# Second layer norms, embedding gates and expert sums with tokens on partitions, and every expert weight split finished on DVE

## The reference, cut to what matters

```python
x = _layer_norm(ALPHA * x + merged @ w_out[i], ln1_g[i], ln1_b[i])      # first norm
if i == 0:
    f = _swiglu(x, ffn_w1[0], ffn_w3[0], ffn_w2[0])                     # dense, 2816 hidden
else:
    f = moe_swiglu(x, ...)       # 8 experts of 3584 hidden, 2 per token, weighted by gates
ple = jax.nn.sigmoid(x @ w_ple_gate[i]) * (p[i] @ w_ple[i])             # embedding and its gate
x = _layer_norm(ALPHA * x + f + ple, ln2_g[i], ln2_b[i])                # second norm
```

## Time and profile before

| | |
|---|---|
| time, median of 3 runs | 2164.01 us (2162.94 to 2166.07) |
| profiled execution: its time | 2165.63 us |
| profiled execution: span from first to last instruction | 2163.8 us |
| TensorE busy | 2093.7 us, 97% of the span |
| VectorE busy | 1458.6 us, 67% |
| ScalarE busy | 966.4 us, 45% |
| GpSimd busy | 350.3 us, 16% |
| mean granted TensorE clock | 0.985 of full speed |
| bytes moved | 553.32 MB, 256 GB/s over the span |

### The profile page before, as it was taken

How to read it: one execution, slowest core, us unless ns; L and a number is a source line. 1 busy time by engine, 2 the same in 40 slices (tenths; PEclk the granted TensorE clock), 3 DMA queues, 4 the chain that set the end, 5 groups by cost and what they waited for, 6 DMA issues and landing times.

```text
span 2163.8 us, 28939 instructions
## 1 busy us (share of the span) xinstructions
PE 2093.7 (97%) x11722; PEld 1801.5 (83%) x11722; DVE 1458.6 (67%) x1415; ACT 966.4 (45%) x1029; POOL 350.3 (16%) x99
## 2 busy tenths in 40 slices
PE   8999999999999989999999999999999979989998
PEld 8877899998877878888888888888888858768998
DVE  4332677664333588898888888888988942346765
ACT  0133210002133257777877777777777732341000
POOL 1001200000001132222232222232224310100000
PEclk9999999999999989999999999999999999999999
DMA  9633579652613468999999999999999963324520
GB/s 350 216 132 104 164 260 326 231 175 79 235 64 117 156 242 328 369 384 385 370 388 367 385 369 388 366 380 368 386 385 386 375 212 122 117 78 156 195 98 20
DMA packets 175854, 553.32 MB, mean 256 GB/s; under 512 B 9248, under 2 KB 97952, under 8 KB 132368
## 3 DMA queue, kind: packets, MB, share of 16 engines
q1 hardware_dynamic: 166928, 517.55, 65.3%
q10 hardware_dynamic: 6912, 25.02, 2.8%
q0 software_dynamic: 1920, 9.40, 1.2%
HBM read 528.09 MB, written 23.59 MB: 255 GB/s over the span
## 4 chain that ended last, share of the span: by engine, by line
PE 91%; DVE 6%; issue 1%; ACT 1%; DMA 0%; DVEq 0%; SPq 0%; ACTq 0%
PE act_ps L1036 26%; PE dve_ps L1061 13%; PE act_ps L859 12%; PE act_ps L964 9%; PE dve_ps L964 9%; PE dve_ps L859 8%; PE job_ps L997 6%; DVE weights_rest L2059 3%; PE job_ps L1044 1%; PE job_ps L911 1%; PE job_ps L930 1%; PE act_ps L1172 1%; PE job_ps L942 1%; PE dve_ps L1377 1%; PE job_ps L1377 1%
## 5 line engine op out<-in xcount | busy, mean ns | idle before, releaser
L2059 DVE TENSOR_TENSOR weights_rest<-weight_ring,expert_short 128x2048 fp32r<-128x2048 f32 x280 | 775.2, 2809 | 110.2 <-ACT expert_short L1545 110.2
L1545 ACT ACTIVATE expert_short<-weight_ring 128x2048 fp32r<-128x2048 f32 x336 | 641.2, 1918 | 104.4 <-PE act_ps L1036 70.7
L748 POOL TENSOR_TENSOR weights_rest<-weight_ring,expert_short 128x2048 fp32r<-128x2048 f32 x56 | 269.2, 4808 | 677.2 <-ACT expert_short L1545 677.2
L1036 PE MATMUL act_ps<-expert_short,tokens_short 128*128 128x512 f32 x896 | 356.2, 397 | 3.9 <-DVE tokens_rest L2069 3.9
L1036 PE MATMUL act_ps<-weights_rest,tokens_short 128*128 128x512 f32 x896 | 351.0, 392 | 0.0
L1036 PE MATMUL act_ps<-expert_short,tokens_rest 128*128 128x512 f32 x896 | 350.8, 392 | 0.0
L1450 ACT ACTIVATE arena_mla<-act_ps 128x256 f32<-128x256 f32 (+1 forms) x80 | 32.6, 407 | 409.1 <-PE act_ps L964 345.5
L1036 PEld LDWEIGHTS act_ps<-expert_short,tokens_short 128*128 128x128 f32 x896 | 169.5, 189 | 38.2 <-DVE weights_rest L2059 4.2
L1036 PEld LDWEIGHTS act_ps<-expert_short,tokens_rest 128*128 128x128 f32 x896 | 169.4, 189 | 36.7
L1036 PEld LDWEIGHTS act_ps<-weights_rest,tokens_short 128*128 128x128 f32 x896 | 169.6, 189 | 33.8
L1988 DVE TENSOR_TENSOR weights_rest<-weight_ring,ffn_weights_short 128x2048 fp32r<-128x2048 f32 x66 | 151.3, 2292 | 2.3
(11 more groups left out here) (325 smaller groups left out, 3718.9 us busy)
## 6 DMA issues: line engine op xcount, KB each, us to landing
weight_ring<-in_moe_w SPq DMA_DIRECT2D x336, 1024.0 KB, 7.2
weight_ring<-in_w_in SPq DMA_DIRECT2D x44, 1024.0 KB, 7.4
weight_ring<-in_ffn_w SPq DMA_DIRECT2D x32, 1024.0 KB, 6.9
weight_ring<-in_w_out SPq DMA_DIRECT2D x12, 1024.0 KB, 6.3
weight_ring<-in_w_gate SPq DMA_DIRECT2D x11, 1024.0 KB, 5.4
weight_ring<-in_w_up SPq DMA_DIRECT2D x11, 1024.0 KB, 8.0
weight_ring<-in_w_down SPq DMA_DIRECT2D x10, 1024.0 KB, 7.1
weight_ring<-in_w_ple_gate SPq DMA_DIRECT2D x8, 1024.0 KB, 6.5
```

The costliest lines, as they stand in the source:

```text
L748: nc.gpsimd.tensor_tensor(ring_lo[slot][:, half], ring[:, slot, half], shorts[u % SHORTS][:, :], ALU.subtract)\
L1036: m = nc.tensor.matmul(bank[0:CAP, :], a[:, 4 * c + k, :], w[:, k, :], start=(c == k == i == 0), stop=(c == 1 and k == 3 and i == 2))
L1545: nc.scalar.activation(shorts[u % SHORTS][:, :], ring[:, slot, half], ACT.Copy).then_inc(moe_w_short, 1)
L2059: V.tensor_tensor(ring_lo[slot][:, half], ring[:, slot, half], shorts[u % SHORTS][:, :], ALU.subtract)\
```

## The change

Three things are laid out with tokens on partitions, two tiles of 128 tokens x 1024 features, in the same buffer `z` (now also viewed as `z_rows`):

1. The `w2` units of the dense network (`swiglu(..., by_rows=True)`) and the embedding gate (`ple_rows`) have the tokens stationary and 512 weight columns moving, 24 matmuls a unit. The embedding product is 4 tiles of 128 x 512 instead of 8 of 128 x 256. ACT scales `x`, turned by TensorE (`turn_x`, which layer 1 had already for its token rows), by ALPHA into `z_rows`; DVE adds gate times embedding.
2. The second norm (`rows_norm`) takes its statistics on DVE with `bn_stats` and `bn_aggr` along the row, ACT makes the root of a 128 x 1 column, DVE normalises, and TensorE turns the rows back (`turn_rows`, 16 transposes). Gain and bias are applied while the turned tiles are read: on ACT in layer 0, on DVE in layer 1, where ACT squares `x` beside it. In layer 0 the last `w2` unit reports its banks one by one (`acc_ready`).
3. The expert rows that POOL fetched are weighed and added straight into `z_rows` (no `ROWS_TURNED`, no `ROWS_ADDED`); expert 7's own rows are placed by a product of the other orientation. All rest parts of expert weights are DVE's; POOL keeps only the fetches, which now wait for a count of finished units.

```diff
-def by_pool(u):
-
-    return u % SHORTS == 3
...
-ROWS_SUMMED, ROWS_TURNED, ROWS_ADDED = (14, 26), (18, 30), (20, 32)
+ROWS_SUMMED = (14, 26)
...
+            def turn_rows(l, banks):
+
+                for i in range(QT):
+                    for j in range(DT):
+                        if j % 4 == 0:
+                            pe.wait_ge(rows_normed, 4 * l + 2 * i + j // 4 + 1)
+                        m = nc.tensor.transpose(banks[j // 2][:, j % 2 * SEQ + i * P:j % 2 * SEQ + (i + 1) * P],
+                                                z_rows[:, i, j * P:(j + 1) * P], const("ident"))
+                        if i == QT - 1 and j % 2:
+                            m.then_inc(rows_turned, 1)
...
+            def ple_rows(l, after, beside=None):
+
+                for i in range(4, 8):
+                    block, c, _ = layer_units(l)[i]
+                    pe.wait_ge(*layer_unit_split(l, i))
+                    short, rest = tiles(ff_w[i % 2][:, :], 4), tiles(ring_lo[block % SLOTS][:, c * 2048:(c + 1) * 2048], 4)
+                    if c == 0:
+                        banks = [act_bank(), act_bank()]
+                    for r, bank in enumerate(banks):
+                        for k in range(4):
+                            if i < 6 and r == 0:
+                                pe.wait_ge(*after(4 * c + k))
...
+                        for b in range(4 if by_rows else 0):
+                            r, half = slice(b // 2 * P, (b // 2 + 1) * P), slice(b % 2 * 512, (b % 2 + 1) * 512)
+                            for k in range(2):
+                                for i, (w, h) in enumerate(((short, 0), (short, 1), (rest, 0))):
+                                    m = nc.tensor.matmul(acc_ps[b][:, :], ff_h[h][:, pair % 4, k, r], w[:, k, half],
+                                                         start=(pair == k == i == 0), stop=(2 * pair + k == f_tiles - 1 and i == 2))
+                            if 2 * pair + 2 == f_tiles and b < 3:
+                                m.then_inc(acc_ready, 1)
...
+            def rows_norm(l, summed):
+
+                for i in range(QT):
+                    for b in (2 * i, 2 * i + 1):
+                        dve.wait_ge(*summed(b))
+                        part = z_rows[:, i, b % 2 * 512:(b % 2 + 1) * 512]
+                        V.tensor_tensor(part, part, acc_ps[b][:, :], ALU.add).then_inc(z_ready, 1)
+                    for b in (2 * i, 2 * i + 1):
+                        dve.wait_ge(z_ready, 4 * l + b + 1)
+                        m = V.bn_stats(row_stats[:, 6 * b:6 * b + 6], z_rows[:, i, b % 2 * 512:(b % 2 + 1) * 512])
+                    step(m)
+                    V.bn_aggr(row_mean[:, 2 * i:2 * i + 2], row_stats[:, 12 * i:12 * i + 12]).then_inc(row_spread, 1)
+                    dve.wait_ge(row_roots, QT * l + i + 1)
+                    for b in (2 * i, 2 * i + 1):
+                        part = z_rows[:, i, b % 2 * 512:(b % 2 + 1) * 512]
+                        V.tensor_scalar(part, part, row_mean[:, 2 * i:2 * i + 1], row_root[:, i:i + 1], ALU.subtract, ALU.mult)\
+                            .then_inc(rows_normed, 1)
...
                         dve.wait_ge(y_picked, 32 * (QT * turn + i + 1))
-                        V.tensor_scalar(x_rows, x_rows, g[:, i:i + 1], None, ALU.mult).then_inc(y_weighed, 1)
+                        V.scalar_tensor_tensor(own, x_rows, g[:, i:i + 1], own, ALU.mult, ALU.add).then_inc(y_weighed, 1)
                         dve.wait_ge(y_weighed, QT * turn + i + 1)
-                        V.scalar_tensor_tensor(x_rows, side_rows[:, :], g[:, 2 + i:3 + i], x_rows, ALU.mult, ALU.add)\
+                        V.scalar_tensor_tensor(own, side_rows[:, :], g[:, 2 + i:3 + i], own, ALU.mult, ALU.add)\
                             .then_inc(y_summed, 1)
```

More of the change, by code:

```diff
@@ L966, in split_product, with merged_tiles @@
                 return m
-            def layer_tiles(l, first, what, x_parts, after, beside=None):
-                for i in range(first, first + 4):
+            def merged_tiles(l, after):
+                for i in range(4):
                     block, c, _ = layer_units(l)[i]
@@ L974, in layer_tiles @@
                     for j in range(2):
-                        bank = act_bank() if what == "A" else dve_bank()
-                        split_product(bank[:, 0:SEQ], w, slice(j * P, (j + 1) * P), x_parts,
-                                      after if i == first and j == 0 else None)\
-                            .then_inc(act_tile_ready if what == "A" else dve_tile_ready, 1)
-                        if beside and i == first and j == 0:
+                        split_product(dve_bank()[:, 0:SEQ], w, slice(j * P, (j + 1) * P), merged_parts,
+                                      after if i == j == 0 else None).then_inc(dve_tile_ready, 1)
@@ new lines, in merged_tiles @@
+                n.block += 2
+            def ple_rows(l, after, beside=None):
[9 more added lines that the diff above has]
+                                pe.wait_ge(*after(4 * c + k))
+                            for p, (a, w) in enumerate(((0, short), (1, short), (0, rest))):
+                                m = nc.tensor.matmul(bank[:, :], ff_x[a][:, 4 * c + k, r * P:(r + 1) * P], w[:, k, :],
+                                                     start=(c == k == p == 0), stop=(c == 1 and k == 3 and p == 2))
+                        if c:
+                            m.then_inc(act_tile_ready, 1)
+                        if beside and i == 4 and r == 0:
@@ L980, in layer_tiles, with turn_x @@
                             beside()
+                    if c == 0:
+                        m.then_inc(ple_unit_used, 1)
                 n.block += 2
-            def swiglu(f_tiles, after):
+            def turn_x(l):
+                for i in range(QT):
+                    for half in range(2):
+                        bank = act_bank()
+                        for k in range(4):
+                            m = nc.tensor.transpose(bank[:, k * P:(k + 1) * P], x[:, 4 * half + k, i * P:(i + 1) * P], const("ident"))
+                        m.then_inc(act_tile_ready, 1)
@@ L985, in swiglu @@
+            def swiglu(f_tiles, after, by_rows=False):
                 units = ffn_units(f_tiles, n)
@@ L1233, in _ @@
                     m.then_inc(dve_tile_ready, 1)
-                    for i in range(QT):
-                        for half in range(2):
-                            bank = act_bank()
-                            for k in range(4):
-                                m = nc.tensor.transpose(bank[:, k * P:(k + 1) * P],
-                                                        x[:, 4 * half + k, i * P:(i + 1) * P], const("ident"))
-                            m.then_inc(act_tile_ready, 1)
+                    turn_x(l)
                     def places():
@@ L1832, in per_tile, with layer_norm @@
                 return a.unsqueeze(1).to_broadcast([P, count, SEQ])
[L1834 removed]
+            def layer_norm(l):
                 bank = ready()
```

272 lines of the change are left out of this document (130 added, 142 removed).

## The result

The changed kernel takes 2126.84 us (median of 4 runs, 2126.14 to 2127.99), the kernel before beside it 2163.48 (2157.91 to 2166.07): a ratio of 0.9842, with an interval of 0.982 to 0.9864. A second series of five runs gave 2126.42 and 0.9835 (0.9819 to 0.9851). The forecast was 2124, in a range of 2112 to 2142: 40.2 us saved, where the medians have 36.6. The profiled execution has a span of 2125.4 us, 38.4 less than before, and it is on these 38.4 that the terms are compared.

The account below looks back on a forecast made before the run. TensorE, busy 97% of the span, was taken as the bound, with DMA close behind in the experts. Nine savings summed to 40.2 us, from 2164.0 to 2123.8, so 2124 us; range for 8 in 10: 2112 to 2142.

Parts of the forecast that it names:

- the likeliest case: Whole kernel: all terms near their size, 2116 to 2133 us, chance 0.55.
- memory took nothing back: Rival, experts: 377 GB/s is the limit, so gains in loop and start return as weight waits; 2134 us, chance 0.15.
- DVE didn't become the bound: Rival, experts: the mean rest stays at 2.81 us, an expert costs DVE 128.2; 2204 us, chance 0.04.
- neither norm kept half of its cost: Rival, both second norms: two-pass statistics and issue stands not covered, 6.5 and 2.2 us less gain; 2133 us, chance 0.15.
- Dense w2 units: Layer 0's dense network: 11 units at 5.44 instead of 5.76 us, 3.5 us saved.
- layer 0's gate: Gate of layer 0: earlier end offset by turn_x, DVE cuts unit 1 sooner; 1.6 us saved, 0 to 3.
- Second norm, layer 0: Last dense matmul to layer 1's first product: 12.1 us becomes 5.4, 6.7 saved, between 4.5 and 8.
- tile 0 is normalised at T + 0.6: Layer 0's second norm: first token tile normalised 0.6 us after the end of the last matmul, T.
- Into the experts: Start of the experts: 4.2 us wait goes, first unit starts some 1.0 later; 3.2 us saved.
- The wait of 4.2: Start of the experts: TensorE's 4.2 us wait for `hidden` goes once POOL makes no rests.
- Experts: Expert stage: first expert 2.2 us saved without the stand, seven loop experts 4.9, last expert 3.1.
- Second norm, layer 1: Last expert unit to `w_in_2`: 31.9 us becomes 17.4, 14.5 saved; 8 if statistics cost 1.24 and issue waits reappear.

Follow-up runs that it names:

- Experiment 4: Changed kernel with each bn_stats of the second norm made twice, once into a spare place: 2130.46 us.
- experiment 9: The changed kernel again as it is, beside other versions on one chip: 2126.42 us.
- Experiment 6: Changed kernel, start of the experts reordered: ACT's short part of the tokens and DVE's rest of the tokens go ahead of unit 1's: 2123.09 us.
- experiment 1: Kernel before with only one part of the change, all rests of expert weights on DVE, POOL keeping only fetches: 2143.18 us.
- experiment 2: Changed kernel with POOL making the rest of every sixth unit again: 2136.38 us.
- experiment 3: Changed kernel, POOL also making pairs of 128 x 1024 subtractions on a buffer of its own in experts 0 to 6, nobody waiting: 2167.22 us.
- experiment 8: Kernel before without the code of the second pass over the experts, on all engines: 2147.75 us.
- experiment 11: Changed kernel without the code of the second pass over the experts: 2127.99 us.
- experiment 12: Kernel before with all rests on DVE and without the code of the second pass: 2141.98 us.
- experiment 10: Changed kernel with the second norm's additions and statistics bank by bank and scalings last, timed a second time: 2120.35 us.
- experiment 5: Changed kernel with the second norm's additions and statistics bank by bank for all four banks, scalings last: 2120.6 us.

## Why the prediction was right, and where it wasn't

*The time.* 2124 forecast, 2126.8 measured; the likeliest case came in, and of the rivals none: memory took nothing back, DVE didn't become the bound, and neither norm kept half of its cost. The largest miss of a term is 2.4, and part of the fit is luck: the misses add up to 7 us without their signs, and the experts' 2.4 too little stood against five terms that were too much.

*Dense w2 units and layer 0's gate.* 3.5 forecast, 3.6 measured: the rows of both forms in the old trace were right, and the 0.06 us a unit that the prediction worked out from issue gaps alone was too little by a factor of five. Layer 0's gate was forecast at 1.6 and gave nothing. The 0.9 of the table is where the gate happened to begin, which moves from one trace to the next (262.8 to 266.1 us in versions with the same code up to there); counted from the first norm it is 0.2 lost. The wait that the forecast wanted gone is gone, 1.5 us before unit 2. In its place TensorE waits before the gate, for ACT's read of a bank of the embedding product. Before and now:

```profile
PE act_ps L964 <- DVE weights_rest L1988: 1.5, 1, 1.5
```

```profile
PE act_ps L980 <- ACT probsT L1461: 0.9, 1, 0.9
```

The forecast counted one such wait inside the gate (0.7, measured 0.8) and not this one. So, counted the same way, the gate ended 1.0 early and not 2.8, and `turn_x` took 2.7 after it.

*Second norm, layer 0.* 5.4 us forecast, 6.3 measured. `bn_stats` was sized exactly (0.60). The step that was off is "tile 0 is normalised at T + 0.6": its statistics wait for bank 1's addition and then for ACT's root, so it is done at T + 1.0. That 0.4 passes on to tile 1, whose own pass took 0.1 more and its transposes and hand-overs 0.4 more than forecast. Experiment 4 shows that tile 0's statistics are on the path.

*Into the experts.* Two things were missed here. "The first unit starts some 1.0 later" was too small: TensorE comes to it 1.9 later, counted from layer 1's start, while the gate's shorter form was to give 0.5 back. Of this 1.5 are in the wait for the rest of the tokens (5.4 for 3.9): I had counted ACT's read of one bank, and not that both rests of DVE and the gate's addition now queue behind it ahead of `tokens_rest`. Another 0.9 is the wait for ACT's read of the embedding bank, as in layer 0. The size isn't sharp: in experiment 9 the same code lost about 1 over this stretch and not 1.9. Experiment 6 changed the order and got 2.2 of the wait back. The wait of 4.2 went as forecast. That POOL slows DVE's rests is shown by experiments 1 to 3, and that this wait comes of it by experiments 1 and 8. But "22 us for six because POOL runs at the same time" hid that it was two collisions, the second by a small margin ahead of `hidden`; experiment 8 lost one of them without touching either engine's work, and with POOL's rests back in the changed kernel (experiment 2) the wait of 4.2 didn't return.

*Experts.* 12.6 measured for 10.2. The forecast took each wait of 0.7 as 0.7 lost. It was 0.88: a loop expert is 118.60 and not 118.8, though the clock was full in that window before as well. The likely reason is how the profile draws matmuls of 512 columns, one every 0.227 us but each 0.39 long: at a wait the overhang of the last one, 0.16, counts as busy. The first expert is 3.6 shorter and not 2.9 (122.2 from its first turn of `hidden` to the next expert's, now 118.6), and the last one 3.5 and not 3.1.

*Second norm, layer 1.* 13.6 for 14.5. The path and the covered stand came as said; what was missed is how much of the gain is the stand. The forecast read its price from the two stands alone, 4.7. Experiments 8, 11 and 12 split it: without the second pass's code the old norm takes 23.1 to 23.7 and the new one 18.2. So in the kernel before some 8 us of the 31.9 were the stands on "issue" with the low clock after them (6 in experiment 12, where the stand was one of 3.4), and the new form of the norm is worth 5. In the changed kernel TensorE begins its transposes at 1735.03, 0.6 behind DVE's end with the first tile, and is through with them before the second tile is ready, so the code costs nothing. The rule on taken branches in the Trainium skill ("Runtime: NRT & Kernel Launch", section "Instruction fetch mechanics") agrees with the stand: it comes and goes with the branch and the code that it skips. That it is a fetch is not shown by these runs.

*What the medians hold beside it.* The same code of the hybrid layer takes 374.3 to 379.2 us in these traces, by its granted clock. The traces of the two kernels compared here both have 0.90 there, so the table is free of it. Several experiments aren't: 3.5 of the 6 us of experiment 10 lie there. Why a version gets one clock or the other is open. The moment at which the stage begins doesn't decide it: w_in_2 at 1745.24 (experiment 11) went with 0.90 and at 1745.88 (experiment 5) with 0.95.

*What the kernel before's own times say.* Its 41 runs fall into two groups, 14 at 2155 to 2160 and 27 at 2162 to 2166, some 6.5 us apart, and the forecast started from a trace of the upper one. The changed kernel's nine runs all lie within 2125.7 to 2128.0. Against the lower group the change is worth some 31 us and not 37. Only the versions in which POOL makes rests have two such groups (the kernel before and experiments 2 and 8), and 6.5 is about what the late `hidden` costs at the start, 4.2 and the lower clock after it. That the groups are the two orders of POOL and DVE of experiment 8 is therefore likely, but not shown, since only one run of each version was traced.

## What to carry to other kernels

When two engines share elementwise work on SBUF, compare the mean of one operation with the least one: a mean of 2.81 us where 2.29 is needed was 146 us of DVE's time, and giving the second engine's sixth of the work to the first made the first less busy. When such a meeting is decided by tenths of a microsecond, the same kernel can have two times, and one trace shows only one of them. When an edit puts one more read on an engine, follow everything that is queued behind it up to the next thing that the bound engine waits for. And when less than one per cent is at stake, compare by place in the trace, at equal granted clocks, before a median is read as the worth of an edit.

## What the runs showed of the hardware that was not expected

- DVE and POOL don't share gradually. In the kernel before 207 of 280 rests meet no operation of POOL and take 2.27 to 2.29 us. A rest that meets POOL's subtraction of two SBUF inputs (4.63 us alone) takes up to 6.7, about the sum of both, and POOL's own up to 6.7 as well. The Trainium skill, "SBUF — State Buffer", says that the port pair the two share is an exclusive lock held for a whole instruction and that the loser fully blocks; the trace agrees, and adds the price here: 2.6 us of DVE's time per operation of POOL, and 2.8 per pair of operations of half the size that touch no data of DVE (experiment 3).
- The stand behind the skipped branch isn't TensorE's alone. In experiment 2 the chain has 3.8 us on "issue" on DVE at the start of the norm, in experiment 6 3.67 on ACT. With the low clock after TensorE's stand it cost the kernel before 6 to 8 us.
- The granted clock of a stage can differ from version to version by 0.90 to 0.97, in code that is the same. For two versions it came again in a second trace: 379.1 us in the hybrid layer for the changed kernel and 375.6 for the other order of the norm, twice each.
